# Mixture-of-experts stage: 32-slot experts on four column quarters, a 64-slot first expert, and 2 MB ring slots filled by two transfers

## The reference, cut to what matters

```python
logits = (xf @ w_router + b_router)            # 256 x 32
top_v, top_i = lax.top_k(logits, 4)            # each token goes to 4 of 32 experts
w = softmax(top_v)
xs = xf[tok]                                   # 1024 rows, sorted by expert
h = ragged_dot(xs, w_up, sizes) + b_up         # 1024 -> 2048 per expert
g, lin = split(h, 2);  g = min(g, 7);  lin = clip(lin, -7, 7)
act = g * sigmoid(1.702 * g) * (lin + 1)
y = ragged_dot(act, w_down, sizes) + b_down    # 1024 -> 1024
out = segment_sum(y * w, tok)
```

## Time and profile before

| | us |
|---|---|
| timed runs, median of 3 | 1978.66 (1978.01 to 1981.87) |
| profiled execution, span from the first to the last instruction | 1976.88 |
| PE busy | 1923.0 (97%) |
| PE weight loads busy | 1189.1 (60%) |
| DVE busy | 744.8 (38%) |
| ACT busy | 453.2 (23%) |
| moved by DMA | 543.47 MB, of which the experts are 402.65 |
| stage of the experts, first up to last down | 958 to 1927 |

### The profile page before, as it was taken

One profiled execution on the slowest core, in us unless ns is written; L12 is line 12 of the kernel. 1 busy time (PEld: TensorE's weight loads), 2 busy tenths in 40 slices (PEclk: granted clock), 3 DMA queues, 4 the chain that ended last, 5 costly groups with the idle time before them and its releaser, 6 DMA issues.

```text
span 1976.9 us, 24271 instructions
## 1 busy us (share of the span) xinstructions
PE 1923.0 (97%) x9570; PEld 1189.1 (60%) x9570; DVE 744.8 (38%) x1058; ACT 453.2 (23%) x668; POOL 12.7 (1%) x19
## 2 busy tenths in 40 slices
PE   6999999999999999999999999999999999999997
PEld 4789899797498889775634434344343444434433
DVE  3555567674365551262222222222222222122233
ACT  1444456212244431062201001010010101001003
POOL 0000000000000000000000000000000000000000
PEclk9999999999999999899899999999999999999999
DMA  9355541201354561114599999999999999999990
GB/s 397 143 202 211 198 169 46 86 0 63 151 224 177 207 270 48 43 43 184 208 387 422 419 414 421 412 422 418 413 419 411 422 419 412 418 413 422 407 419 36
DMA packets 67816, 543.47 MB, mean 275 GB/s; under 512 B 7552, under 2 KB 7552, under 8 KB 10528
## 3 DMA queue, kind: packets, MB, share of 16 engines
q1 hardware_dynamic: 65584, 534.58, 66.1%
q0 software_dynamic: 1872, 6.82, 1.0%
q10 hardware_dynamic: 288, 1.05, 0.1%
HBM read 541.37 MB, written 1.05 MB: 274 GB/s over the span
## 4 chain that ended last, share of the span: by engine, by line
PE 92%; DVE 4%; ACT 2%; DMA 1%; issue 1%; POOL 0%; DVEq 0%; ACTq 0%; POOLq 0%
PE ps L2119 17%; PE ps L2105 11%; PE ps L2134 9%; PE ps L520 6%; PE ps L2148 6%; PE ps L632 3%; PE ps L631 3%; PE ps L630 3%; PE ps L1201 3%; PE ps L704 3%; PE ps L706 3%; PE ps L705 3%; PE ps L1412 2%; PE ps L2195 2%; PE ps L1965 1%; PE ps L2178 1%
## 5 line engine op out<-in xcount | busy, mean ns | idle before, releaser
L2119 PE MATMUL ps<-ring,arena 128*64 128x512 f32 x1536 | 334.9, 594 | 0.0
L2119 PEld LDWEIGHTS ps<-ring,arena 128*64 128x64 f32 x1536 | 108.1, 137 | 214.4 <-issue 214.4
L759 DVE TENSOR_TENSOR ring_split<-ring,ring_split 128x1024 fp32r<-128x1024 f32 x156 | 187.1, 1222 | 124.8 <-ACT ring_split L811 124.6
L2369 DVE TENSOR_SCALAR arena<-ps 128x512 f32<-128x512 f32 x40 | 27.7, 692 | 538.8 <-PE ps L2119 287.7
L2105 PE MATMUL ps<-ring,arena 128*128 128x512 f32 x512 | 223.3, 594 | 0.0
L811 ACT CAST ring_split<-ring 128x1024 fp32r<-128x1024 f32 x156 | 160.5, 1047 | 163.1 <-PE ps L706 88.6
L2134 PE MATMUL ps<-ring,arena 128*64 128x512 f32 x768 | 170.1, 595 | 0.0
L2105 PEld LDWEIGHTS ps<-ring,arena 128*128 128x128 f32 x512 | 97.8, 191 | 116.8 <-issue 115.4
L2519 ACT ACTIVATE arena<-arena 128x512 f32<-128x512 f32 x40 | 25.2, 631 | 575.3 <-DVE arena L2369 575.3
L704 PE MATMUL ps<-arena_split,ring_split 128*128 128x256 f32 x512 | 143.8, 281 | 0.3 <-DVE ring_split L759 0.3
L705 PE MATMUL ps<-arena_split,ring_split 128*128 128x256 f32 x512 | 142.9, 279 | 0.0
(11 more groups left out here) (388 smaller groups left out, 2398.8 us busy)
## 6 DMA issues: line engine op xcount, KB each, us to landing
ring<-experts_dram SPq DMA_DIRECT2D x384, 1024.0 KB, 10.5
ring<-weights_dram SPq DMA_DIRECT2D x57, 2048.0 KB, 12.1
row_buf<-rows_dram POOLq DMA_DIRECT2D x13, 512.0 KB, 8.6
ring<-weights_dram SPq DMA_DIRECT2D x3, 1024.0 KB, 11.2
tab<-tables_dram SPq DMA_DIRECT2D x1, 2287.0 KB, 17.5
x<-tokens_dram SPq DMA_DIRECT2D x1, 1024.0 KB, 5.0
arena<-rows_dram SPq DMA_DIRECT2D x2, 512.0 KB, 19.0
xT<-weights_dram SPq DMA_DIRECT2D x1, 1024.0 KB, 7.1
```

Source lines behind the costliest of these rows:

```text
L759: V.tensor_tensor(low, raw, high, ALU.subtract).then_inc(sem("part_low"), 1)
L2119: ins = T.matmul(bank(first_bank + m)[at:at + SMALL], xs[:, 2 * c + d, P + SMALL * (j - 1):P + SMALL * j], w[half_][:, d, m * STEP:(m + 1) ...
```

## The change

The rooms of a group become 64, 32, 128, 32 slots, in steps called mid, tiny 1, large, tiny 3. The group's total of slots goes from 320 to 256. Expert 0 keeps step 0, which is now a 64-slot one; the eight busiest others get the 128-slot steps, the next seven the 64-slot ones, the last sixteen 32 slots each. Experts that don't fit lead to three more passes instead of one.

A tiny expert's up product uses four column quarters of the array: each of four matmuls in a row has the same 32 stationary columns, writes to its own 32 partitions of one PSUM bank, and streams 256 gate and 256 linear columns. Its down product puts even and odd blocks of the contraction on different quarters, and the combine adds them. Its clip, sigmoid and products are 256 wide instead of 512, and its turn has two transposes instead of four. Its bias and its one-hot spread take two matmuls with two pick tables (`half_even`, `half_odd`).

The ring has six slots of 2 MB instead of twelve pieces of 1 MB. A slot is filled by two transfers of 1 MB, each with a semaphore of its own, and is given back once, when all of it is read. The weights are laid out in DRAM in units of 128 rows of 16 KB, of which each transfer reads 8 KB per row. In the large step the down of the tiny one before lies between the two halves of the up; the large expert's down follows in the step after.

```diff
-SMALL = 64
-BIGS = 8
+SMALL, TINY = 64, 32
 GROUPS, STEPS_OF = 8, 4
+MID, TINY_1, LARGE, TINY_3 = range(STEPS_OF)
+ROOMS = (SMALL, TINY, P, TINY)
+PASSES = 4
...
-    big = k % STEPS_OF == 0
-    t["room"] = np.broadcast_to(np.where(big, P, SMALL)[None, :], (P, EXPERTS))
-    place = np.where(big, k // STEPS_OF, BIGS + 3 * (k // STEPS_OF) + k % STEPS_OF - 1)
+    g, j = k // STEPS_OF, k % STEPS_OF
+    t["room"] = np.broadcast_to(np.array(ROOMS)[j][None, :], (P, EXPERTS))
+    place = np.select([k == 0, j == LARGE, j == MID], [0, 1 + g, GROUPS + g], 2 * GROUPS + 2 * g + j // 2)
...
-    up = i["w_up_2"][0].reshape(EXPERTS, 4, 2, P, 2, 2, STEP)
-    up = up.transpose(0, 5, 1, 3, 2, 4, 6).reshape(EXPERTS, 8, P, 2048)
-    down = i["w_down_2"][0].reshape(EXPERTS, 4, 2, P, D).transpose(0, 1, 3, 2, 4).reshape(EXPERTS, 4, P, 2048)
+    up = i["w_up_2"][0].reshape(EXPERTS, 2, 4, P, 2, 2, STEP)
+    up = up.transpose(0, 5, 1, 3, 2, 4, 6).reshape(EXPERTS, 4, P, UNIT)
+    down = i["w_down_2"][0].reshape(EXPERTS, 2, 4, P, D).transpose(0, 1, 3, 2, 4).reshape(EXPERTS, 2, P, UNIT)
...
-        CHUNKS, RING = 12, 12
+        PICKS = {MID: (picks_b[:, 0, :],), TINY_1: (picks_a[:, 0, :], picks_a[:, 1, :]),
+                 LARGE: (picks_b[:, 1, :], picks_b[:, 2, :]), TINY_3: (picks_a[:, 2, :], picks_a[:, 3, :])}
+        PICK_TABLES = {MID: ("half_both",), TINY_1: ("half_even", "half_odd"),
+                       LARGE: ("half_0", "half_1"), TINY_3: ("half_even", "half_odd")}
+        U_MID, U_TINY_1, U_LARGE_A, U_LARGE_B, U_TINY_3 = range(5)
+        CHUNKS, RING = 6, 6
         PASS_CHUNKS = CHUNKS * EXPERTS
-        FIRST = CHUNKS - 4
+        FIRST = CHUNKS - 2
...
-                sp.dma_start(ring_chunk(q_const), experts[e, chunk]).then_inc(sem(f"moe_full{q_const % RING}"), 16)
+                for h in range(2):
+                    part = slice(HALF * h, HALF * h + HALF)
+                    sp.dma_start(ring[:, q_const % RING, part], experts[e, chunk, :, part])\
+                      .then_inc(sem(f"moe_full{q_const % RING}_{h}"), 16)
...
-                up = [(e, A + c) for c in range(4)] + [(e, B + c) for c in range(4)]
-                down = [(last_e, DOWN + c) for c in range(4)]
-                if j == 0:
-                    order = up[:4] + down + up[4:]
+                down = [(last_e, DOWN), (last_e, DOWN + 1)]
+                if j == LARGE:
+                    order = [(e, A), (e, A + 1)] + down + [(e, B), (e, B + 1)]
                 else:
-                    order = [u for c in range(4) for u in (up[c], up[4 + c])] + down
+                    order = [(e, A), (e, B), (e, A + 1), (e, B + 1)] + down
                 for r, (owner, chunk) in enumerate(order):
-                    load(before_step(k) + r, FIRST + r, owner, chunk, wait=not (first and r < 4))
...
+            def up_mid(g, first=False):
+                pe.wait_ge(sem("moe_pick"), cnt(4, g, MID + 1))
+                bias(0, PICKS[MID][0])
                 k = STEPS_OF * g
+                for c in range(2):
+                    if not first:
+                        pe.wait_ge(sem("moe_xs"), later(g, 4 * c + 4))
+                    w = up_view(chunk(k, 2 * c)), up_view(chunk(k, 2 * c + 1))
+                    for d in range(4):
+                        if d == 2:
+                            chunk(k, 2 * c, 1)
+                            chunk(k, 2 * c + 1, 1)
                         for m in range(2):
                             for half_ in range(2):
                                 at = SMALL * half_
+                                ins = T.matmul(bank(m)[at:at + SMALL], xs_of(4 * c + d, MID), w[half_][:, d, m, :],
+                                               start=False, stop=c == 1 and d == 3, skip_group_check=True)
+                                if d == 3 and m == 1:
                                     ins.then_inc(sem("moe_used"), 1)
 
...
+            def up_tiny(g, j):
+
+                pe.wait_ge(sem("moe_pick"), cnt(4, g, j + 1))
+                for r in range(2):
+                    T.matmul(view(bank(0), (2, 256)), PICKS[j][r], bias_pair[:, :, 256 * r:256 * r + 256],
+                             start=r == 0, stop=False, skip_group_check=True)
+                k = STEPS_OF * g + j
+                for c in range(2):
+                    w = up_view(chunk(k, 2 * c)), up_view(chunk(k, 2 * c + 1))
+                    for d in range(4):
+                        if d == 2:
+                            chunk(k, 2 * c, 1)
+                            chunk(k, 2 * c + 1, 1)
+                        for q in range(4):
+                            ins = T.matmul(view(bank(0)[TINY * q:TINY * q + TINY], (2, 256)), xs_of(4 * c + d, j),
+                                           w[q // 2][:, d, :, 256 * (q % 2):256 * (q % 2) + 256],
+                                           start=False, stop=c == 1 and d == 3, skip_group_check=True)
+                            if d == 3 and q >= 2:
+                                ins.then_inc(sem("moe_used"), 1)
+
...
+            def up_large(g, half_):
+                if half_ == 0:
+                    pe.wait_ge(sem("moe_pick"), cnt(4, g, LARGE + 1))
+                bias(2 * half_, PICKS[LARGE][half_])
+                k = STEPS_OF * g + LARGE
+                for c in range(2):
+                    w = up_view(chunk(k, 4 * half_ + c))
+                    for d in range(4):
+                        if d == 2:
+                            chunk(k, 4 * half_ + c, 1)
+                        for m in range(2):
+                            ins = T.matmul(bank(2 * half_ + m), xs_of(4 * c + d, LARGE), w[:, d, m, :],
+                                           start=False, stop=c == 1 and d == 3, skip_group_check=True)
+                    ins.then_inc(sem("moe_used"), 1)
+
...
+            def down_tiny(k, r):
+
+                for c in range(2):
+                    w = down_view(chunk(k, r + c))
+                    for d in range(4):
+                        if d == 2:
+                            chunk(k, r + c, 1)
+                        f = 4 * c + d
+                        for half_ in range(2):
+                            at = TINY * (2 * half_ + f % 2)
+                            ins = T.matmul(bank(4)[at:at + TINY],
+                                           actT[:, 0, f % 2, TINY * (f // 2):TINY * (f // 2 + 1)],
+                                           w[:, d, half_ * STEP:(half_ + 1) * STEP], start=f < 2, stop=f >= 6,
+                                           skip_group_check=True)
+                    ins.then_inc(sem("moe_used"), 1)
+
...
+            def tiny_1(g, first=False):
+                k = STEPS_OF * g + TINY_1
                 if first:
+                    pe.wait_ge(sem("moe_xs_rest"), 4 * n + 4)
+                pe.wait_ge(sem("moe_read"), cnt(5, g, U_MID + 1))
+                up_tiny(g, TINY_1)
+                pe.wait_ge(sem("moe_onehotT"), cnt(4, g, MID + 1))
                 if not first:
                     pe.wait_ge(sem("moe_y_low"), cnt(5, g, 0))
+                    combine_small(1, (2, 3, 5, 7))
                 elif n == 0:
+                    down_bias((2, 3, 5, 7))
+                pe.wait_ge(sem("moe_actT"), cnt(5, g, U_MID + 1))
+                down_mid(k, 4)
+                turn(g, U_TINY_1, 1, 2)
                 summed(k - 2, 3)
+                spread_ranks(TINY_1)
+
+            def large(g):
+                k = STEPS_OF * g + LARGE
+                pe.wait_ge(sem("moe_read"), cnt(5, g, U_TINY_1 + 1))
+                up_large(g, 0)
+                pe.wait_ge(sem("moe_y_low"), cnt(5, g, 1))
+                pe.wait_ge(sem("moe_onehotT"), cnt(4, g, TINY_1 + 1))
+                combine_small(0, (2, 3, 5, 7))
+                pe.wait_ge(sem("moe_actT"), cnt(5, g, U_TINY_1 + 1))
+                down_tiny(k, 2)
+                turn(g, U_LARGE_A, 0)
+                summed(k - 2, 3)
+                up_large(g, 1)
+                spread_ranks(LARGE)
+
+            def tiny_3(g, last=False):
+                k = STEPS_OF * g + TINY_3
+                pe.wait_ge(sem("moe_read"), cnt(5, g, U_LARGE_A + 1))
+                up_tiny(g, TINY_3)
                 pe.wait_ge(sem("moe_y_low"), cnt(5, g, 2))
+                pe.wait_ge(sem("moe_read"), cnt(5, g, U_LARGE_B + 1))
+                pe.wait_ge(sem("moe_onehotT"), cnt(4, g, LARGE + 1))
+                combine_small(1, (2, 3, 1, 7))
+                pe.wait_ge(sem("moe_actT"), cnt(5, g, U_LARGE_A + 1))
+                turn(g, U_LARGE_B, 1)
+                pe.wait_ge(sem("moe_actT"), cnt(5, g, U_LARGE_B + 1))
+                down_large(k, 4)
+                turn(g, U_TINY_3, 0, 2)
                 summed(k - 2, 3)
+                spread_ranks(TINY_3)
...
-                program(eng, 1)
+                for n in range(1, PASSES):
+                    program(eng, n)
```

(46 more changed lines are left out.)

439 lines of the change are left out of this document (187 added, 252 removed).

## The result

The changed kernel takes 1962.99 us (median of 4 runs, 1961.25 to 1963.71) against 1978.63 (4 runs): ratio 0.991, 95% interval 0.9896 to 0.9924. Forecast: 1954, range 1947 to 1972. 15.6 us were gained where 24.7 were forecast. The profiled execution took 1963.31, with a span of 1961.5; the forecast for the span was 1951.8. These 9.7 us are what has to be explained.

A forecast was written before the change was run, and what follows sets the result against it. DMA becomes the bound: 395.3 MB at 422.5 GB/s from 959.2 land by 1894.8; PE's last tiny down ends at 1901.9, and a 49.9 us tail gives a span of 1951.8, carried over to 1954 us; range 1947 to 1972.

The forecast's parts named there:

- What bounds the kernel: Expert groups: PE sets the pace at 120.8 us, DMA follows at 119.1; only 1.7 a group, 14 us in all, winnable.
- PE's work: Expert groups: four column quarters run at once, 0.107 us a record; PE's group falls to 103 us, waits of 3 included.
- The ring keeps DMA fed: 2 MB slots over the experts: 8.4 MB, 20 us, stay issued or landed; PE comes 1 to 2 us late, no hole.
- The end of the stage: Last experts: last byte lands at 1894.8, last tiny up's data at 1874.9, large down ends 1893.4, tiny down 1901.9.
- Bytes flow from 959.2: Start of the expert stage: unchanged, with DMA at full rate counted from 959.2 us.
- The tail stays 49.9: Behind the last expert down: the 49.9 us that follow it in the kernel before stay.
- main case: Whole kernel: DMA becomes the bound, PE has 16 us a group to spare; 1954 us, alone 1948 to 1960; chance 0.68.
- (b): Tiny experts' matmuls: a record takes 0.16 to 0.19 us, ring holes stay; 1965 us; chance 0.07.
- (c): PE's new waits at tiny experts: the clock falls to 1.2 GHz, costing 7 us; 1961 us; chance 0.08.
- (a): Tiny experts' matmuls: column quarters go no better than halves, 0.217 us a record, group 122.6; 1990 us; chance 0.12.
- (d): Expert transfers: half-unit reads, 8 KB rows at 16 KB pitch, run at 405 GB/s, 40 us more; 1994; chance 0.04.
- (e): Expert slots: an expert over its room sets off three more passes of at least 952 us each; chance 0.01.

The follow-up runs named there:

- experiment 1: Each expert transfer brings only half of its columns (4 KB rows), in the changed kernel and in the kernel before: 1822.07 and 1976.99 us.
- experiment 8: Changed kernel with code for two passes over the slots instead of four: 1959.21 us, first up at 956.0.
- experiment 5: Changed kernel with each 2 MB slot filled by one transfer with one semaphore instead of two of each: 1951.90 us, ratio 0.9868.
- experiment 3: Changed kernel with every matmul of the 32-slot ups and downs issued twice: 1984.66 us, ratio 1.0028.
- experiment 4: Changed kernel with expert weights laid out in DRAM so that each 1 MB transfer reads one contiguous block: 1964.01 us, ratio 0.9921.
- experiment 7: Changed kernel with four ple2 matmuls moved behind the last small combine: 1961.33 us; together with one 2 MB transfer and semaphore a slot: 1952.12 us.

## Why the prediction was right, and where its 9.7 us went

**Where the gain came.** The stage's first up starts at 958.14 in the kernel before and at 961.47 in the changed one, the first up of the second group at 1077.43 and 1071.81:
```profile
958.14 2.48 PE L2105 MATMUL ps<-ring,arena 128*128 128x512 f32 x3
...
1077.43 13.89 PE L2105 MATMUL ps<-ring,arena 128*128 128x512 f32 x32
...
1071.81 13.95 PE L2118 MATMUL ps<-ring,arena 128*64 128x512 f32 x64
```
The last down ends at 1926.96 and at 1910.78. So the stretch up to the second group gave 9.0 us and the rest of the stage 10.6; 3.3 were lost ahead of the stage and 0.8 behind it. That is the 15.4 by which the span fell.

**What bounds the kernel.** Right. PE alone held the kernel before (experiment 1), and of the 1.7 us a group that DMA left, 1.5 came: 120.86 to 119.33, 12.2 us if all eight groups gave as much (forecast 14).

**PE's work.** Right: 0.109 us a record, where 0.107 was taken. The Trainium skill's factor for four row tiles ("TensorE: Matmul & The Clock Gate", Part 3, measured speedup) would have made it an estimated 0.140; four column quarters here do better than that. PE's group was 100.66, not 103: of the 3 us for new waits the trace has the 0.68 at the large down and, each group, one like this (PE in order of time, changed kernel):
```profile
1259.16 0.66 PE L2207 MATMUL ps<-tab,arena 128*128 128x128 f32 x4 [0.64 <-DVE arena L2441]
```
It had no consequence, since PE has time to spare.

**The ring keeps DMA fed.** Right: of the 5 us windows from 975 to 1890 none is below 415. The forecast sign, none under 400 after 960, did not quite come true: the windows at 960 and 970 have 228 and 387.

**The end of the stage** is where the sum came out short. The last tiny up, the large down and the tiny down of the changed kernel, and the gate:
```profile
1881.20 5.13 PE L2137 MATMUL ps<-ring,arena 128*32 128x512 f32 x32 [5.53 <-DMA ring<-experts_dram]
...
1888.71 14.00 PE L2199 MATMUL ps<-ring,arena 128*128 128x512 f32 x32 [0.68 <-ACT arena L2588]
...
1905.20 2.08 PE L2222 MATMUL ps<-arena_split 128*128 128x512 f32 x8 [2.03 <-DVE arena_split L2395]
1907.20 3.64 PE L2184 MATMUL ps<-ring,arena 128*32 128x512 f32 x32
...
1918.64 5.17 PE L1953 MATMUL ps<-xT,pleT 128*128 128x512 f32 x8
...
1925.41 27.73 PE L1968 MATMUL ps<-ring,xT 128*128 128x512 f32 x64
```
The forecast had the last tiny up's data at 1874.9, so the last but one of its 1 MB pieces at 1872.4; PE got it at 1881.20, 8.8 later. Four terms make 8.2 of them; the other 0.6 has no place:
- *Bytes flow from 959.2*: from 962.3 (228 GB/s in the window from 960), 3.1 late. *The start: unchanged* was wrong. The executions vary, but the comparison of like with like in experiment 8 puts some 3 us on the changed program; why is open.
- *Full rate from there*: the window at 970 has 387 GB/s, 0.4 us. The first tiny expert's holes are nearly gone, as forecast.
- *422.5 GB/s*: it is 421.7, 1.7 us over 386 MB. I had taken the rate of windows without a hole, 421 and 423, and chose the upper side.
- *Landed when its bytes have moved*: by 1881.20 DMA had moved 387.2 MB since 955 (418 GB/s in that window), 1.3 more than are up to and with this piece, which is 3.0 us. I had no term for the time from when DMA has moved that many bytes to when the engine may go on. The trace can divide it. Each transfer adds 16 to its semaphore, in 16 increments, and PE waits for all; those of this piece come between 1877.08 and 1881.07, on average at 1879.05, and PE starts 0.13 behind the last. An estimate from these: the bytes were moved by 1878.2, so 0.9 us lie between them and the average increment, and 2.0 between the average and the last. So the larger part is that one transfer's increments come 4 us apart, and a wait needs the last. The Trainium skill, "DMA: Bandwidth & Descriptors", Anatomy of one DMA, gives about 2 us as fixed, mostly the receipt of the last write, for transfers that GpSimd issues; these are issued by SP, and by this estimate some 0.9 of the 3.0 could be of that kind.

From there my steps hold: large down's end 1902.55 against 1893.4 (+9.1), tiny down's end 1910.78 against 1901.9 (+8.9). *The tail stays 49.9*: it is 50.7, with the clock at 0.84 and a ple2 pair of 5.17 us for 3.70; in experiment 5, where that pair took 3.70, the tail is 50.0. 8.9 + 0.8 = 9.7.

**Was the range luck?** In part. The measured 1963 lies outside the 1948 to 1960 of the main case alone. The range reached to 1972 for (b) and (c), and neither happened; what filled their room are the late start and the time behind the last bytes, which no term and no rival had.

**The rivals.** (a) had the right sign for the case that didn't come. Its price, 1990 against 1984.7, was near by luck: it put 14 us on the groups, which in experiment 3 are 0.2 shorter than before, and took 3 off for the first expert, where 2.8 were added. (b) no: 0.109 us a record. (c) The low clock came, as the trace of the group shows (0.94 over it), and cost nothing while DMA set the pace: the groups stay at 119.3 to 119.4 with DMA at 422, and experiment 5 runs at 0.94 too and is faster. Its only price is at the end: the tail's 0.8, and some 0.7 of the last tiny up (5.13 us, where at full clock the last piece, 2.5 behind, and 1.9 of work would make 4.4). The section of the Trainium skill that the prediction named for this ("TensorE: Matmul & The Clock Gate", HAM oscillation) forecast the fall rightly; it isn't a loss where the wait, not the work, sets the pace. (d) no: experiment 4. The neighbour of (d) that I didn't have on the list is true, though: *a row read is 8 KB as before* was taken for no cost, which holds against the kernel before; but 2 MB slots allow rows of 16 KB, and by not using them the change left some 11 us. The rows of before had windows at 431 and 442 GB/s, where transfers of 2048 KB run, and I read them only for the clock. (e) did not come either: there is one pass.

Not tried: the ring with two semaphores and 64-slot experts, the ring's part of the change alone.

## What to carry to other kernels

When two resources are both near full, work out each one's time for a unit of work and halve one of them on the chip: the smaller margin is the whole gain, here 1.5 of 20 us a group. Once DMA is the bound, its rate is the thing to tune: longer rows were worth 6 GB/s, and the pieces that let PE start earlier cost more than the earlier start gave. A sum that ends on a transfer needs a term for the time from its bytes to the last of its increments, here 3 us. And a stretch that a change doesn't touch in the source can still take another time, so compare its start in several profiles.

## What the runs showed of the hardware

- A row costs some 9 ns of a DMA engine beside its bytes, an estimate from 428, 422 and 410 GB/s with rows of 16, 8 and 4 KB. Whether 2 MB came in one transfer or two, and a pitch of 8 or 16 KB in memory, didn't matter (422 GB/s each time).
- The 16 increments of one 1 MB transfer in a full queue came over 4 us, and the waiting engine needed the last of them.
- Transfers to partitions 0 to 63 alone run at 206 GB/s, with the DMA engines' busy share at 1.02.
- Matmuls on four column quarters run at nearly four times the pace: 0.109 us for a 128x512 fp32 record, 0.429 at full width.
- One program's executions differ by several us: 1950.0 to 1954.1 in experiment 7, in two pairs, and 1980.8 to 1987.4 in experiment 3.
